# Two attentions of a fused two-layer block: row sums from the exponential, probabilities scaled on ScalarE, transposes two tiles behind the scores

## The reference, cut to what matters

```python
def forgetting_attention(q, k, v, f_logit, b_f):          # first layer, 8 heads
    log_f = jax.nn.log_sigmoid((f_logit + b_f).astype(jnp.float32))
    cum = jnp.cumsum(log_f, axis=1).transpose(0, 2, 1)
    for blk in range(L // Q_BLOCK):                       # 8 blocks of 128 queries
        q0 = blk * Q_BLOCK
        kend = q0 + Q_BLOCK
        s = jnp.einsum('bqhd,bkhd->bhqk', q[:, q0:kend], k[:, :kend]).astype(jnp.float32) * scale
        s = s + cum[:, :, q0:kend, None] - cum[:, :, None, :kend]
        s = jnp.where(k_pos[None, :] <= q_pos[:, None], s, NEG_INF)
        p = jax.nn.softmax(s, axis=-1)
        outs.append(jnp.einsum('bhqk,bkhd->bqhd', p.astype(v.dtype), v[:, :kend]))

def chunk_band_attention(q, k, v, rel_bias):              # second layer, 4 heads
    s = jnp.einsum('bcqhd,bckhd->bchqk', qc, kb).astype(jnp.float32) * (HEAD_DIM ** -0.5)
    s = jnp.where(valid[None, :, None, None, :], s + bias[None, None], NEG_BIG)
    p = jax.nn.softmax(s, axis=-1).astype(v.dtype)
    o = jnp.einsum('bchqk,bckhd->bcqhd', p, vb)
```

## Time and profile before

| what | us |
|---|---|
| median of three executions | 3533.94 |
| the profiled execution | 3534.19 |
| its span, first to last instruction | 3532.2 |
| TensorE busy | 3412.5 (97%) |
| VectorE busy | 1425.0 (40%) |
| ScalarE busy | 873.6 (25%) |
| GpSimd busy | 913.2 (26%) |
| first attention on TensorE, about | 320 to 803.5 |
| second attention on TensorE, about | 1880 to 2124 |

### The profile page before, as it was taken

One profiled execution on the slowest core, in us unless ns is written; L12 is line 12 of the kernel. 1 busy time (PEld: TensorE's weight loads), 2 busy tenths in 40 slices (PEclk: granted clock), 3 DMA queues, 4 the chain that ended last, 5 costly groups with the idle time before them and its releaser, 6 DMA issues. The chain is left out here.

```text
span 3532.2 us, 40721 instructions
## 1 busy us (share of the span) xinstructions
PE 3412.5 (97%) x16184; PEld 2799.5 (79%) x16184; DVE 1425.0 (40%) x1579; ACT 873.6 (25%) x1068; POOL 913.2 (26%) x454
## 2 busy tenths in 40 slices
PE   8999999999999999999999998999999999999997
PEld 6787887887877888888867886877778688888886
DVE  7843566655325221212153445563542521121123
ACT  3222322224323111111132222313342411111112
POOL 2212111112341222222322213331254222222225
PEclk9999999999999999999999999999999999999998
DMA  3435434315322111111224313223263211111113
GB/s 132 149 95 153 142 127 125 108 60 197 130 93 81 48 48 48 48 51 44 101 97 129 100 66 113 78 72 142 99 215 136 78 48 48 47 49 52 48 48 131
DMA packets 101601, 333.42 MB, mean 94 GB/s; under 512 B 11920, under 2 KB 21520, under 8 KB 101328
## 3 DMA queue, kind: packets, MB, share of 16 engines
q1 hardware_dynamic: 100896, 329.52, 27.8%
q10 hardware_dynamic: 576, 2.10, 0.2%
HBM read 249.06 MB, written 85.52 MB: 95 GB/s over the span
## 5 line engine op out<-in xcount | busy, mean ns | idle before, releaser
L278 POOL TENSOR_TENSOR w_lo<-w_raw,w_hi 128x1024 fp32r<-128x1024 f32 (+1 forms) x304 | 698.6, 2302 | 2441.4 <-ACT w_hi L274 2441.1
L318 PE MATMUL pair<-act_hi,w_hi 128*128 128x512 f32 x2976 | 946.2, 399 | 11.2 <-DVE p L605 4.8
L318 PE MATMUL pair<-act_lo,w_hi 128*128 128x512 f32 x2976 | 924.0, 392 | 0.0
L318 PE MATMUL pair<-act_hi,w_lo 128*128 128x512 f32 x2976 | 921.6, 391 | 0.0
L318 PEld LDWEIGHTS pair<-act_lo,w_hi 128*128 128x128 f32 x2976 | 562.0, 189 | 120.4
L318 PEld LDWEIGHTS pair<-act_hi,w_lo 128*128 128x128 f32 x2976 | 561.3, 189 | 120.7
L318 PEld LDWEIGHTS pair<-act_hi,w_hi 128*128 128x128 f32 x2976 | 541.8, 189 | 116.4 <-issue 14.1
L274 ACT CAST w_hi<-w_raw 128x1024 fp32r<-128x1024 f32 x274 | 287.4, 1049 | 870.6 <-PE pair L318 822.4
L605 DVE TENSOR_TENSOR p<-pair,rs 128x1024 f32<-128x1024 f32 x100 | 122.1, 1222 | 370.3 <-PE pair L318 370.1
L1881 DVE TENSOR_TENSOR f2v<-pair,rs 128x1024 f32<-128x1024 f32 x42 | 51.4, 1224 | 332.8 <-PE pair L318 332.8
L318 PE MATMUL pair<-f1hh,w_hi 128*128 128x512 f32 x480 | 147.8, 389 | 0.0
(11 more groups left out here) (480 smaller groups left out, 3980.7 us busy)
## 6 DMA issues: line engine op xcount, KB each, us to landing
w_raw<-in_stream SPq DMA_DIRECT2D x275, 512.0 KB, 3.5
proj<-p SPq DMA_DIRECT2D x101, 512.0 KB, 2.6
m2g<-proj SPq DMA_DIRECT2D x32, 512.0 KB, 4.8
foxx<-proj SPq DMA_DIRECT2D x32, 256.0 KB, 5.7
m1g<-proj SPq DMA_DIRECT2D x16, 512.0 KB, 3.7
x<-f1y SPq DMA_DIRECT2D x16, 512.0 KB, 2.6
act_lo<-x SPq DMA_DIRECT2D x16, 512.0 KB, 6.8
fx_cb<-fox_cum SPq DMA_DIRECT2D x8, 512.0 KB, 7.7
```

The source lines that it names most:

```text
L278: last = nc.gpsimd.tensor_tensor(wlo[:, slot, at:at + n], raw[:, slot, at:at + n], whi[:, slot, at:at + n].bitcast(F32), ALU.subtract)
L318: last = nc.tensor.matmul(out_pair[:, h * HALF:(h + 1) * HALF], wt, a[:, h * HALF:(h + 1) * HALF], start=k == 0 and n_pass == 0, stop=k == ...
```

## The change

The value matrix is stored once, without ones, and both memsets go. The exponential gives the row sums through its accumulator output into a second column of `st`. VectorE takes the reciprocal of that one column, 128 x 1. ScalarE multiplies the tile by it in place (`scaled`). `normalise` becomes `gather`, a plain copy of 64 x 512 out of PSUM for every fourth tile. The tile is now weighed two iterations after its scores instead of one, and `s` and `st` have three slots. At the end of an attention two tiles are left to weigh, with one more `point(1)` between them.

```diff
-            vt = sb(at, name + "vt", [P, 2, 2, NT, P])
-            s, pt = sb(at, name + "s", [P, 2, L]), sb(at, name + "pt", [P, 2, L])
-            o, r = sb(at, name + "o", [P, 2, L]), sb(at, name + "r", [P, HALF])
-            st = sb(at, name + "st", [P, 2, 1])
+            vt = sb(at, name + "vt", [P, 2, NT, P])
+            s, pt = sb(at, name + "s", [P, 3, L]), sb(at, name + "pt", [P, 2, L])
+            o, st = sb(at, name + "o", [P, 2, L]), sb(at, name + "st", [P, 3, 2])
...
-                    A.mark(A.after(ready, weighed.get(h - 3)).copy(vt[:, slot, 0, j0:j0 + 4, 0:HD], four[:, :, 0:HD]))
-                    copied = A.mark(nc.scalar.copy(vt[:, slot, 1, j0:j0 + 4, HD:P], four[:, :, HD:P]))
+                    copied = A.mark(A.after(ready, weighed.get(h - 3)).copy(
+                        vt[:, slot, j0:j0 + 4, :], bank[0][:].rearrange("p (j n) -> p j n", j=4)))
...
+            def scaled(t, h, n, k0, nk, e):
+
+                sum_, w = st[:, t % 3, 1:2], nk * P
+                v = V.mark(V.after(e).reciprocal(sum_, sum_))
+                return A.mark(A.after(v).activation(s[:, t % 3, 0:w], s[:, t % 3, 0:w], ACT.Copy, scale=sum_))
...
-            def normalise(t, h, n):
+            def gather(t, h, n):
...
-                mine, sums = (slice(0, HD), slice(HD, P)) if h % 2 == 0 else (slice(HD, P), slice(0, HD))
-                slot = h // 2 % 2
-                V.mark(V.after(pv_done[t]).reciprocal(r[mine, :], bank[1][sums, :]))
-                state["o_read"] = V.mark(V.then(out_in.get(h // 2 - 2)).tensor_tensor(
-                    o[mine, slot, n // 4 * HALF:(n // 4 + 1) * HALF], bank[1][mine, :], r[mine, :], ALU.mult))
+                mine, slot = slice(h % 2 * HD, (h % 2 + 1) * HD), h // 2 % 2
+                state["o_read"] = V.mark(V.after(pv_done[t], out_in.get(h // 2 - 2)).tensor_copy(
+                    o[mine, slot, n // 4 * HALF:(n // 4 + 1) * HALF], bank[1][mine, :]))
...
                 scores[h] = ready = PE.mark(last)
-                if pend:
-                    weigh(*pend)
+                if ready_p:
+                    weigh(*ready_p)
+                drained = ready_p
+                if exped:
+                    ready_p = (*exped[:-1], scaled(*exped))
...
-                if pend:
-                    normalise(*pend[0:3])
-                x = A.mark(A.after(x).activation(sc, sc, ACT.Exp, bias=st[:, sl, :]))
-                pend = (t, h, n, k0, w // P, x)
+                if drained:
+                    gather(*drained[0:3])
+                x = A.mark(A.after(x).activation(sc, sc, ACT.Exp, bias=st[:, sl, 0:1], accum_out=st[:, sl, 1:2]))
+                exped = (t, h, n, k0, w // P, x)
...
-            weigh(*pend)
-            normalise(*pend[0:3])
+            weigh(*ready_p)
+            gather(*ready_p[0:3])
+            ready_p = (*exped[:-1], scaled(*exped))
+            point(1)
+            weigh(*ready_p)
+            gather(*ready_p[0:3])
```

More of the change, by code:

```diff
@@ L690, in attention @@
             qh, ql, ks = (sb(at, name + n, [P, 2, L], F32R) for n in ("qh", "ql", "ks"))
-            vt = sb(at, name + "vt", [P, 2, 2, NT, P])
-            s, pt = sb(at, name + "s", [P, 2, L]), sb(at, name + "pt", [P, 2, L])
-            o, r = sb(at, name + "o", [P, 2, L]), sb(at, name + "r", [P, HALF])
-            st = sb(at, name + "st", [P, 2, 1])
+            vt = sb(at, name + "vt", [P, 2, NT, P])
+            s, pt = sb(at, name + "s", [P, 3, L]), sb(at, name + "pt", [P, 2, L])
+            o, st = sb(at, name + "o", [P, 2, L]), sb(at, name + "st", [P, 3, 2])
             bias, bias_in, bias_fixed = head_bias(at)
-            G.mark(G.then().memset(vt[:, :, 0, :, HD:], 1.0))
-            ones_in = G.mark(G.then().memset(vt[:, :, 1, :, 0:HD], 1.0))
             arrived, bias_ready, split, scores, biased, values_in, weighed = {}, {}, {}, {}, {}, {}, {}
@@ L739, in values @@
                     v_read[h] = ready
-                    four = bank[0][:].rearrange("p (j n) -> p j n", j=4)
-                    A.mark(A.after(ready, weighed.get(h - 3)).copy(vt[:, slot, 0, j0:j0 + 4, 0:HD], four[:, :, 0:HD]))
-                    copied = A.mark(nc.scalar.copy(vt[:, slot, 1, j0:j0 + 4, HD:P], four[:, :, HD:P]))
+                    copied = A.mark(A.after(ready, weighed.get(h - 3)).copy(
+                        vt[:, slot, j0:j0 + 4, :], bank[0][:].rearrange("p (j n) -> p j n", j=4)))
                     if j0 == 0:
@@ L754, in weigh @@
                 state["copied"] = transposes(pt[:, sl, :].rearrange("p (j n) -> p j n", n=P),
-                                             lambda j: s[:, sl, j * P:(j + 1) * P], nk, P, e, free=state["copied"],
+                                             lambda j: s[:, t % 3, j * P:(j + 1) * P], nk, P, e, free=state["copied"],
                                              after=lambda: point(1 if nk > 4 else 1.5))
-                PE.after(state["copied"], values_in[h], ones_in, state["o_read"])
+                PE.after(state["copied"], values_in[h], state["o_read"])
                 for j in range(nk):
-                    last = nc.tensor.matmul(bank[1][:, n % 4 * P:(n % 4 + 1) * P], vt[:, h // 2 % 2, h % 2, k0 // P + j, :],
+                    last = nc.tensor.matmul(bank[1][:, n % 4 * P:(n % 4 + 1) * P], vt[:, h // 2 % 2, k0 // P + j, :],
                                             pt[:, sl, j * P:(j + 1) * P], start=j == 0, stop=j == nk - 1)
@@ L782, in attention @@
             state["copied"] = values(0, None)
-            pend = None
+            exped, ready_p = None, None
             for t, (h, n) in enumerate((h, n) for h in range(heads) for n in range(NT)):
                 q0, k0, k1 = tiles[n]
-                w, sl = k1 - k0, t % 2
+                w, sl = k1 - k0, t % 3
                 if n == 0:
@@ L798, in attention @@
                 scores[h] = ready = PE.mark(last)
-                if pend:
-                    weigh(*pend)
+                if ready_p:
[3 more added lines that the diff above has]
+                    ready_p = (*exped[:-1], scaled(*exped))
                 sc = s[:, sl, 0:w]
-                V.after(ready, bias_ready[h], pv_done[t - 2] if t > 1 else None)
+                V.after(ready, bias_ready[h], pv_done[t - 3] if t > 2 else None)
                 state["scores_read"] = add_bias(sc, wide[:, 0:w], bias[:, h % 2, :], q0, k0, k1)
                 biased[h] = V.last()
-                V.mark(V.then().reduce_max(st[:, sl, :], sc, AX.X))
-                x = V.mark(V.then().tensor_scalar(st[:, sl, :], st[:, sl, :], -1.0, None, ALU.mult))
-                if pend:
-                    normalise(*pend[0:3])
-                x = A.mark(A.after(x).activation(sc, sc, ACT.Exp, bias=st[:, sl, :]))
-                pend = (t, h, n, k0, w // P, x)
+                V.mark(V.then().reduce_max(st[:, sl, 0:1], sc, AX.X))
+                x = V.mark(V.then().tensor_scalar(st[:, sl, 0:1], st[:, sl, 0:1], -1.0, None, ALU.mult))
+                if drained:
+                    gather(*drained[0:3])
+                x = A.mark(A.after(x).activation(sc, sc, ACT.Exp, bias=st[:, sl, 0:1], accum_out=st[:, sl, 1:2]))
+                exped = (t, h, n, k0, w // P, x)
                 if n == 4 and h + 1 < heads:
```

## The result

The changed kernel takes 3518.80 us (median of six executions, 3516.53 to 3522.94), the kernel before 3531.80 us in its six (3526.49 to 3534.83). The ratio is 0.9966 with a 95% interval of 0.9953 to 0.9978, so the change saves 13 us (by the interval, 8 to 17).

What follows compares the result with a forecast made beforehand. TensorE was taken as the bound, busy 3412.5 of 3532.2 us. Gains of 11.9 + 2.7 + 5.0 + 3.4 less a cost of 4.6 gave 18.4 us, so 3534.2 became 3516 us, range 3507 to 3528.

Steps and rivals of the forecast that it cites:

- VectorE's work: Both attentions: VectorE loses 80.5 us of reciprocals, gains 14.8 of small ones, 65.7 us less; alone worth nothing.
- The junctions and their clock: First attention, between heads: shorter TensorE waits and no low clock (2.4 us) save 11.9 us in all.
- The second attention: TensorE's bias waits there, 5.6 us less the 2.9 at its start that stays: 2.7 us saved.
- The merge: After the first attention: loads go out earlier, saving 3.35 us of wait and 1.7 of low clock, 5.0 together.
- The recurrence: After the second attention: its chain starts earlier without the last reciprocal of 3.35 us, taken as 3.4 us saved.
- The starts: Start of each attention: new idle of 2.0 and 1.1 us, next bias 0.3, low clock 1.2; cost 4.6 us.
- The lag: First attention: transposes an iteration later remove 1.8 us of waiting for the exponential; scaling hidden by a 2.6 us margin.
- ScalarE's additions: Both attentions: a scaling per tile, 1.152 us for 128 x 1024, and 0.1 per accumulator output; some 70 us, off the path.
- A: Junctions of heads: split collisions with GpSimd replace the reciprocal, 20.3 us come back, 3536 us; chance 0.13.
- B: Merge and recurrence absorb their gains of 5.0 and 3.4 us, starts cost all their bounds, 3527 us; chance 0.13.
- C: Score tiles: a ring between ScalarE and VectorE outlasts TensorE's iteration, 3564 us, or 3552 in milder form; chance 0.07.
- D: More than forecast: another clock loss saved (1.35 us), starts cost only 1.5, other short waits vanish, 3510 us; chance 0.12.

Runs made afterwards that it cites:

- e8: The kernel before, lag of one tile kept, with every normalise replaced by a plain copy and outputs not divided by row sums: 3513.10 us, ratio 0.9947.
- e1: The kernel before, with only the last normalise of each attention made a plain copy, not divided by its row sums: 3527.92 us, ratio 0.9987.
- e2: The kernel before with only the lag of two tiles and three score slots; reciprocal and multiply stay: 3524.31 us, ratio 0.9975.
- e3: The changed kernel with the lag taken back to one tile, new normalisation kept: 3569.06 us, ratio 1.0101 to the kernel before.
- e7: The changed kernel with each tile scaled twice on ScalarE, the second time by 1.0: 3522.51 us, ratio 0.9972 to the kernel before.
- e6: The changed kernel with three background points of tile 0's weighing moved ahead of the scores of tiles 1 and 2: 3506.09 us, ratio 0.9924 to the kernel before.
- e9: e6 with the transposes of the next values issued ahead of the scaling and exponential on ScalarE's queue: 3503.82 us, ratio 0.9920 to the kernel before.

## Why the prediction was right, point by point

- *The forecast.* 18.4 us less was forecast, 13.0 were measured by the medians and 15.0 between the two profiled executions; 3518.80 us lies in the range of 3507 to 3528. The causes are the ones named, and the sum was too hopeful by 3.4 us of the profile. Of these, 1.3 are the clock ahead of the first scores, 1.3 are missing at the junctions, 0.8 at the starts and 0.5 each at the second attention and the merge; the recurrence and the remaining stretches give 1.0 back. Two terms came out near their numbers partly by luck, as said below.
- *VectorE's work.* 66 us less, as worked out. The copy takes 0.69 us, the value taken. The small reciprocal takes 0.16 us (0.15 taken).
- *The junctions and their clock.* 11.9 us forecast; 11.2 less 0.6 for the moved scores, 10.6 measured. e8 shows that the reciprocal in the queue was the cause. The parts fit less well than the sum. The low clock was worth 2.5 us as forecast, but TensorE's idle time fell by 6.4 us and not by 9.5. Another 1.7 us lie in its busy time without a lowered clock, and what they are is open. What I missed are new waits: 1.45 us for a copy of the values that stands behind the exponential, 0.84 behind a convolution, 1.07 at a junction where ScalarE's casts are late.
- *The second attention.* 2.7 us of idle time forecast; 2.8 less 0.6, 2.2 measured. The number is near by luck. The idle time fell by 0.4 us only: the sum of the bias waits rose, because the start gained one, and small ones of 0.33 us came behind late evictions, where the small reciprocal stands in front of the bias. The other 1.8 us are nearly all the stretch of low clock, which e1 lacks with the old code.
- *The merge.* 5.0 forecast, 4.5 measured, including the clock. The first wait fell by 3.7 us and the second, which I had not counted, rose by 0.6. e1 shows the cause.
- *The recurrence.* 3.4 forecast, 3.8 measured. In e1 the same edit gave 2.3. In the ten kernels whose second attention ends with the copy this stretch takes 48.5 to 50.5 us, and 52.55 and 53.33 in the two that end with the reciprocal (the kernel before and e2). So the direction is sure and the size is known only as 2 to 4 us against before.
- *The starts.* 4.6 forecast. The table has 7.8; less 1.2 for the moved scores and less the 1.3 ahead of the first scores, 5.4 are the change's. The idle was as forecast (1.99 for 2.0, 0.97 for 1.1). What was mis-sized is the lowered clock, about 2.4 us (1.4 and 1.1), where I had taken 0.6 us for each start and 0.3 for a next bias. By comparison of profiles the second start is known only to about 1 us: from the value transposes to PV first the old order takes 18.75 to 20.04 us in four profiles.
- *The lag.* I wrote that the 1.8 us of waiting for the exponential go because transposes come later, and that is true, but it is the smallest thing that the lag does. e3 shows that without it the scaling would cost 46.6 us of waits. The prediction put the scaling at nothing because of a margin of 2.6 us in each iteration; it had not looked at the queue in front of the small reciprocal.
- *ScalarE's additions.* 71 us as the rows said. The accumulator read is an instruction of its own of 0.19 us, within the bounds and above the 0.1 taken.
- *Rivals.* A: all splits of both attentions took 1.22 to 1.23 us in the changed kernel; the one collision of the earlier trace rows, the only one among the splits before, is gone. B: the merge and the recurrence did gain. C: e7 speaks against it, but only with the lag: e3 is 35 us slower than the kernel before. D did not come.

## What to carry to other kernels

Where one engine is busy all the time and all queues are in order, price an instruction on another engine by what stands behind it in its queue at the moments when the busy engine waits, not by its sum: 80 us of reciprocals were worth some 19 (e8), and in e3 one of 0.16 us, late in its queue, was behind a wait of 6.5 us. In this kernel a longer chain between two engines was safe only with enough distance to cover the queue in front of its shortest member. At the start of the pipeline the distance had to be filled with other work (e6), or it showed twice, as idle and as lowered clock.

## What the runs showed of the hardware

- A reciprocal of 64 x 512 from PSUM takes 3.35 us, nearly five times a multiply or a copy of the same shape (0.69).
- ScalarE's scaling by a column takes the same time as the exponential of the same shape (1.153 and 1.145 us for 128 x 1024), and no table load stands between them: each attention shows one, ahead of its first exponential. An accumulator output adds a row of 0.19 us.
- The low clock behind the same wait has no fixed length. From the value transposes to the first scores TensorE runs the same instructions in eleven of these kernels; it took 4.92 to 5.09 us in four of them (the kernel before, e1, e6, e9) and 6.10 to 6.43 us in the seven others. Behind a wait of 1.74 us in the second attention the clock fell in the kernel before (granted 0.66 from 2045 to 2050 us) and not in e1 (1.00 from 2040 to 2045 us). Why is open; it makes a stretch of a single profile uncertain by 1.3 to 1.6 us.
